# PEER block of a hybrid layer: 44 of the down tiles beside top-k, 12 between the gate products with low parts on VectorE, 8 behind them

## The chip, the cores and the metric

One core of one Trainium2 chip. The metric is device time in microseconds (us), the median over several executions; the kernel before takes 3331.22 us (three runs, 3329.69 to 3335.95).

## What is computed

The program is two layers on 512 tokens of width 1024 (a mixer with a PEER layer, then attention with a mixture of experts). The change is within the PEER layer. The part of the reference that matters:

```python
q = (xt @ w_query).reshape(t, PEER_HEADS, PEER_DKEY)            # 8 heads, 2 x 128
s1 = einsum("thd,hkd->thk", q1, sub_keys_1); s2 = ...           # 128 keys each
v1, i1 = top_k(s1, 16); v2, i2 = top_k(s2, 16)
top_s, pos = top_k(v1[..., :, None] + v2[..., None, :], 16)     # 16 of 256 pairs a head
gate = softmax(top_s)                                           # 128 (expert, gate) pairs a token
act = gelu(einsum("td,thkd->thk", x, w_down[expert])) * gate    # 16384 experts
y = einsum("thk,thkd->td", act, w_up[expert])
```

## The kernel before

For the first 128 tokens the 128 pairs of a token are gathered one by one. For the other 384 (TD) the layer is computed densely: the 16384 experts are 128 tiles of 128 experts, and each down tile is the product of a 128x1024 block of w_down with the tokens, followed by a gelu. Half of these tiles (STEPS = 64) are computed ahead, in otherwise different stages, and are written to the DRAM tensor `early`; the other half is computed in the experts stage itself, which reads one early tile and one block of gates at each of its 64 steps. Full precision comes from splitting each operand in a rounded high part (ScalarE) and a low part (the difference), so a down tile costs 24 matmuls: 8 blocks of the inner dimension times hi*hi, hi*lo, lo*hi (`part` or `product`).

*Score stage* (`stage_retrieve`, L1164). TensorE computes 68 tiles in the order of the list `order`: 16 query tiles ("q"), in four units of four, with 6 down tiles ("e") after each of the first three units and 34 after the last, SCORED = 52 in all. ScalarE evicts a tile (L1342 query, L1347 gelu), and splits the tile four further on (L1323); GpSimd makes the low parts (L1264); SP loads the next tile when a low part is done and saves groups of four tiles to `early`. VectorE meanwhile does the top-k of each unit (L1402 to L1467). It needs ScalarE for an Exp (L1363), which stands behind the eviction of the tiles in `exp_at` and waits for the centred scores (L1443); the sums (L1419) follow in the next unit. After the product of tile TILES - 4 TensorE transposes the picks for the next stage (L1316).

*Gates stage* (`stage_gate_matrix`, L1479). From the picks a matrix of gates, experts by tokens, is made for every token: VectorE writes two sets of 128x128 rows (L1517, one instruction for the four tokens of a group; L1520, three instructions; the fourth is made by ScalarE, L1575 distance and L1581 tent), TensorE multiplies them (L1544) into one of four banks of PSUM, ScalarE takes the bank to `out` (L1588). 16 groups make a batch (a 4 MB store by SP, L1645), and there are six batches with two buffers. Between the products 12 down tiles are computed, two in each batch: four of the tile's 24 matmuls (L1555) in each group but the first four; split (L1570) and gelu (L1566) on ScalarE, low part on GpSimd (L1530), the load at L1624, the save of the gelu's result at L1628. Four of the early tiles are loaded to `c.hid` at the start (L1632) for the first steps of the experts stage, with two blocks of w_up and of w_down.

*Experts stage* (`stage_peer_experts`, L1654). Its first matmul (L1749) waits for the split (L1792) and the low part (L1871) of its first tile.

A stage ends when SP has waited for all its transfers; the semaphores are then cleared behind a barrier of all engines (`Stage.__exit__`). An engine executes in the order of its program, and a wait holds all that is behind it. The semaphores of the change: `wd_h` counts splits, `wd_l` low parts, `h_done` finished tiles, `gelued` gelus, `taken` banks taken to `out`, `g_done` groups multiplied, `saved` and `stashed` finished stores.

## Time and profile before

| | |
|---|---|
| median of the runs | 3331.22 us |
| the profiled execution's own span | 3332.1 us |
| TensorE busy | 3127.5 us (94%) |
| VectorE busy | 2668.2 us (80%) |
| ScalarE busy | 1817.5 us (55%) |
| GpSimd busy | 834.3 us (25%) |
| score stage | about 554 to 876 us |
| gates stage | about 881 to 1054 us |
| experts stage | about 1055 to 1850 us |

In the profile PE is TensorE's matmuls, PEld its weight loads, DVE VectorE, ACT ScalarE, POOL GpSimd, SP the queue that issues most transfers; L1520 is line 1520 of the kernel. A name such as gates_hot is a tile of the program, `out<-in` names what an instruction writes and reads. Busy shares are means over stages with different bounds; a change in one stage is read from that stage.

### The profile page before, as it was taken

Reading aid. Unit: us, or ns where it says so; the run is one execution under the profiler, and the core shown is the slowest. Engines: PE = TensorE matmul, PEld = TensorE weight load, DVE = VectorE, ACT = ScalarE, POOL = GpSimd, SP = SyncE. Lnnn points to the kernel's source line nnn. Section 1 sums busy time; section 2 is a strip of 40 time slices with the busy share of each in tenths; the row PEclk is TensorE's granted clock in tenths of the full one; section 3 lists DMA queues with packets and bytes.
Section 4 is the critical chain, followed back from the end, with each engine's and each line's share of the span. In section 5 each row is a group of like instructions: output and inputs, shape, how many; then the busy total and the mean of one; then the engine's idle time right before and its main releaser. Section 6 shows DMA issues by size and latency. Waiting matters only on the chain. (4 is left out here: it accounts for less than half of the span.)

```text
span 3332.1 us, 47952 instructions
## 1 busy us (share of the span) xinstructions
PE 3127.5 (94%) x16376; PEld 2708.8 (81%) x16376; DVE 2668.2 (80%) x3821; ACT 1817.5 (55%) x2211; POOL 834.3 (25%) x516
## 2 busy tenths in 40 slices
PE   7999788999887999999999888799999999999998
PEld 7996677999887888888888766688888888888885
DVE  6895652995496887878888565899999999999997
ACT  4433442334585333333333344578877777877775
POOL 0000102445321444445545100211211211211212
PEclk9999888999998999999999889899999999999999
DMA  5231031335456998999998414699999999999996
GB/s 142 70 83 39 1 127 64 136 119 175 152 228 250 337 343 320 350 341 331 344 358 318 170 29 165 257 364 356 366 368 354 361 371 363 364 373 367 365 371 252
DMA packets 195750, 853.24 MB, mean 256 GB/s; under 512 B 21776, under 2 KB 104336, under 8 KB 151936
## 3 DMA queue, kind: packets, MB, share of 16 engines
q1 hardware_dynamic: 167712, 700.86, 57.4%
q0 software_dynamic: 27936, 151.02, 11.1%
q8 instruction: 64, 1.05, 0.1%
q14 instruction: 38, 0.31, 0.0%
HBM read 810.39 MB, written 59.24 MB: 261 GB/s over the span
## 5 line engine op out<-in xcount | busy, mean ns | idle before, releaser
L3207 DVE TENSOR_TENSOR moe_w_lo<-all_raw,moe_w_hi 128x2048 fp32r<-128x2048 f32 x298 | 676.2, 2287 | 50.6 <-ACT moe_w_hi L3133 48.2
L3133 ACT ACTIVATE moe_w_hi<-all_raw 128x2048 fp32r<-128x2048 f32 x298 | 569.3, 1916 | 80.0 <-PE moe_GU L3072 60.0
L3072 PE MATMUL moe_GU<-moe_w_hi,moe_x_lo 128*128 128x512 f32 x1056 | 412.3, 390 | 0.0
L3071 PE MATMUL moe_GU<-moe_w_lo,moe_x_hi 128*128 128x512 f32 x1056 | 412.2, 390 | 0.0
L3070 PE MATMUL moe_GU<-moe_w_hi,moe_x_hi 128*128 128x512 f32 x1056 | 411.7, 390 | 0.0
L1889 DVE SCALAR_TENSOR_TENSOR experts_pair<-experts_pair,all_x_first 128x1024 f32<-128x1024 f32 x128 | 156.4, 1222 | 142.6 <-DMA experts_pair<-in_peer_pairs,experts_slot 142.6
L1733 POOL DMA_INDIRECT experts_pair<-in_peer_pairs,experts_slot x128 | 222.4, 1738 | 114.7 <-POOL experts_slot L1730 110.0
L1264 POOL TENSOR_TENSOR score_w_lo<-all_hT,score_w_hi 128x1024 fp32r<-128x1024 f32 x67 | 165.2, 2467 | 303.7 <-DVE all_x_lo L1380 161.4
L1730 POOL COPY experts_slot<-all_pair_id 128x1 uint32 x128 | 152.8, 1194 | 334.1 <-DVE all_h L1901 304.4
L2976 POOL DMA_INDIRECT pair_rows<-all_mixT,all_slot x32 | 48.8, 1526 | 738.2 <-ACT all_mixT L3175 738.2
L3071 PEld LDWEIGHTS moe_GU<-moe_w_lo,moe_x_hi 128*128 128x128 f32 x1056 | 198.6, 188 | 42.1
L3072 PEld LDWEIGHTS moe_GU<-moe_w_hi,moe_x_lo 128*128 128x128 f32 x1056 | 198.6, 188 | 41.7
L3070 PEld LDWEIGHTS moe_GU<-moe_w_hi,moe_x_hi 128*128 128x128 f32 x1056 | 199.0, 188 | 40.6
L3207 DVE TENSOR_TENSOR moe_w_lo<-all_hT,moe_w_hi 128x2048 fp32r<-128x2048 f32 x98 | 222.5, 2284 | 0.1
L3080 PE MATMUL moe_Y<-moe_w_hi,moe_hid_hi 128*128 128x512 f32 x528 | 212.3, 402 | 0.8 <-DVE moe_hid_lo L3237 0.8
L3082 PE MATMUL moe_Y<-moe_w_hi,moe_hid_lo 128*128 128x512 f32 x528 | 206.2, 391 | 0.0
L3081 PE MATMUL moe_Y<-moe_w_lo,moe_hid_hi 128*128 128x512 f32 x528 | 205.8, 390 | 0.0
L3133 ACT ACTIVATE moe_w_hi<-all_hT 128x2048 fp32r<-128x2048 f32 x98 | 187.7, 1915 | 32.5 <-PE moe_GU L3072 18.7
L1749 PE MATMUL experts_H<-all_x_hi,experts_wd_hi 128*128 128x384 f32 x512 | 173.6, 339 | 20.0 <-DVE experts_wd_lo L1871 19.9
L1288 PE MATMUL score_H<-all_x_hi,score_w_hi 128*128 128x384 f32 (+1 forms) x544 | 190.3, 350 | 1.4 <-DVE all_x_lo L1380 1.4
L1290 PE MATMUL score_H<-all_x_hi,score_w_lo 128*128 128x384 f32 (+1 forms) x544 | 189.6, 349 | 0.0
L1289 PE MATMUL score_H<-all_x_lo,score_w_hi 128*128 128x384 f32 (+1 forms) x544 | 189.6, 349 | 0.0
(546 smaller groups left out, 8108.7 us busy)
## 6 DMA issues: line engine op xcount, KB each, us to landing
all_raw<-in_w_moe SPq DMA_DIRECT2D x149, 2048.0 KB, 9.8
all_hT<-in_w_moe SPq DMA_DIRECT2D x49, 2048.0 KB, 9.7
all_hT<-in_peer_wdT SPq DMA_DIRECT2D x128, 512.0 KB, 8.8
all_wu<-in_peer_pairs SPq DMA_DIRECT2D x64, 1024.0 KB, 10.5
peer_gates<-gates_out SPq DMA_DIRECT2D x6, 4096.0 KB, 11.6
experts_gt<-peer_gates SPq DMA_DIRECT2D x32, 768.0 KB, 9.7
all_hT<-in_w_in SPq DMA_DIRECT2D x40, 512.0 KB, 3.8
all_hid<-peer_early SPq DMA_DIRECT2D x60, 192.0 KB, 7.6
```

The lines of the kernel that those rows point to most:

```text
L1288: pe.matmul(out, left, c.x_hi[:, k, at:T], start=(k == 0), stop=False)
L1289: pe.matmul(out, left, c.x_lo[:, k, at:T], start=False, stop=False)
L1290: mm = pe.matmul(out, low, c.x_hi[:, k, at:T], start=False, stop=(k == KD - 1))
L1733: pool.indirect_dma_start(out=pair[:, v, :], out_offset=None, in_=a["peer_pairs"][:, :], in_offset=bass.IndirectOffsetOnAxis(ap=slot[:, n: ...
L3070: pe.matmul(out, x_hi[:, kx, :], hi[:, k, :], start=False, stop=False)
L3071: pe.matmul(out, x_hi[:, kx, :], lo[:, k, :], start=False, stop=False)
L3072: mm = pe.matmul(out, x_lo[:, kx, :], hi[:, k, :], start=False, stop=(kx == KD - 1))
L3080: pe.matmul(Y[:, b, :], hid_hi[:, h, :], hi[:, f, cols], start=(h == 0), stop=False)
L3081: pe.matmul(Y[:, b, :], hid_hi[:, h, :], lo[:, f, cols], start=False, stop=False)
L3082: mm = pe.matmul(Y[:, b, :], hid_lo[:, h, :], hi[:, f, cols], start=False, stop=(h == KD - 1))
L3133: act.activation(w_hi[p % RING][:], piece_of(r, p), ACT.Copy).then_inc(w_high, 1)
L3207: dve.tensor_tensor(w_lo[p % RING][:], piece_of(r, p), w_hi[p % RING][:].bitcast(F32), ALU.subtract).then_inc(w_low, 1)
```

## The change

SCORED falls from 52 to 44, so the score stage has 60 tiles, and the third and fourth Exp stand at tiles 39 and 47 in place of 43 and 56. The first four early tiles (DIRECT) are no longer computed there but last of all, in the gates stage, where their gelus write `c.hid` itself; the load of `c.hid` is gone.

In the gates stage 12 tiles are still computed between the group products (LOOPED), now six matmuls in each odd group and none in the even ones. Their low parts are made by VectorE, after the hot rows of groups 5 and 13 of each batch, but the very first, which stays on GpSimd. ScalarE's program is unrolled; a gelu and a split stand after take 0 and after take 8 of each batch. SP issues a load ahead of the saves of the batch before, and one behind them.

Behind the last group's products come 8 tiles more (TAIL), 24 matmuls each in one piece. Their raw weights are loaded during the last batch, six of them to the part of `out` that holds the last but one batch, once that is stored; four gelus go to what is left of it and are saved, four stay in `c.hid`. The store of the last batch is issued behind these loads and behind the saves of tiles 10 and 11.

```diff
-SCORED = 52
+SCORED = 44
+DIRECT = 4
-    exp_at = {18: 0, 29: 1, 43: 2, 56: 3}
+    exp_at = {18: 0, 29: 1, 39: 2, 47: 3}
-                    sp.dma_start(w[:, i % R, :], (wq_d if kind == "q" else wd_d)[n]).then_inc(w_in[i % R], 16)
+                    sp.dma_start(w[:, i % R, :], wq_d[n] if kind == "q" else wd_d[DIRECT + n]).then_inc(w_in[i % R], 16)
-                    sp.dma_start(c.early[g * G:(g + 1) * G].rearrange("j p t -> p j t"), stash[:, g % 2, :, :]).then_inc(stashed[g % 2], 16)
+                    sp.dma_start(c.early[DIRECT + g * G:DIRECT + (g + 1) * G].rearrange("j p t -> p j t"), stash[:, g % 2, :, :]).then_inc(stashed[g % 2], 16)
...
-    assert SCORED + 2 * BATCHES == STEPS and 2 * 3 * KD == 4 * (TB // U - R)
+    LOOPED, TAIL = 2 * BATCHES, 8
+    TILES = LOOPED + TAIL
+    FIRST = DIRECT + SCORED
+    KEPT = TILES - DIRECT
+    assert FIRST + LOOPED + TAIL - DIRECT == STEPS and 2 * 3 * KD == 6 * (TB // U) // 2 and BATCHES % 2 == 0
...
+        spare = out[:, 0, :, :].rearrange("p i t -> p (i t)")
+        queued = spare[:, 0:(TAIL - 2) * D].rearrange("p (j n) -> p j n", n=D)
+        kept = spare[:, (TAIL - 2) * D:(TAIL - 2) * D + DIRECT * TD].rearrange("p (j t) -> p j t", t=TD)
...
+        def tile(t):
+            return FIRST + t if t < KEPT else t - KEPT
+
+        def raw(t):
+            return wd[:, t % 2, :] if t < LOOPED + 2 else queued[:, t - LOOPED - 2, :]
+
+        def bent(t):
+            if t < LOOPED:
+                return stash[:, t % 2, :]
+            return kept[:, t - LOOPED, :] if t < KEPT else c.hid[:, t - KEPT, :]
...
-                with dve.Fori(0, TD // (R * U)) as it:
-                    for u in range(R):
-                        at = dve.snap(it * (R * U) + u * U)
-                        dve.wait_ge(g_done, it * R + (u + 1))
+                with dve.Fori(0, BATCHES) as b:
+                    for g in range(per * R):
+                        u = g % R
+                        at = dve.snap(b * TB + g * U)
+                        dve.wait_ge(g_done, b * (per * R) + (g + 1))
...
+                        if g == 5:
+                            dve.wait_ge(wd_h, b * 2 + 2)
+                            low(1, wd[:, 1, :])
+                        if g == 13:
+                            dve.wait_ge(wd_h, b * 2 + 3)
+                            low(0, wd[:, 0, :])
+                for t in range(LOOPED + 1, TILES):
+                    dve.wait_ge(wd_h, t + 1)
+                    low(t % 2, raw(t))
...
-                with pool.Fori(0, BATCHES) as b:
-                    for v in range(2):
-                        pool.wait_ge(wd_h, b * 2 + (v + 1))
-                        pool.wait_ge(gelued, b * 2 + (v + 1))
-                        pool.tensor_tensor(wd_lo[:, v, :], wd[:, v, :], wd_hi[:, v, :].bitcast(F32),
-                                           ALU.subtract).then_inc(wd_l, 1)
+                pool.wait_ge(wd_h, 1)
+                pool.tensor_tensor(wd_lo[:, 0, :], wd[:, 0, :], wd_hi[:, 0, :].bitcast(F32), ALU.subtract).then_inc(first_l, 1)
...
-                    for i in range(per):
-                        for u in range(R):
-                            n = b * (per * R) + (i * R + u)
...
-                            if i == 0:
-                                continue
-                            for q in range(4 * (R * (i - 1) + u), 4 * (R * (i - 1) + u) + 4):
-                                v, k, kind = q // (3 * KD), q // 3 % KD, q % 3
-                                if q % (3 * KD) == 0:
-                                    pe.wait_ge(wd_l, b * 2 + (v + 1))
-                                    pe.wait_ge(gelued, b * 2 + (v + 1))
...
-                                    mm.then_inc(h_done, 1)
+                    for g in range(per * R):
+                        u = g % R
+                        n = b * (per * R) + g
+                        pe.wait_ge(weighed, n + 1)
+                        pe.wait_ge(tented, n + 1)
+                        pe.wait_ge(taken, n + 1)
...
+                        mm.then_inc(g_done, 1)
+                        if g % 2 == 0:
+                            continue
+                        v = g // 8
+                        if g % 8 == 1:
+                            pe.wait_ge(first_l, 1)
+                            pe.wait_ge(wd_l, b * 2 + (v + 1))
+                            pe.wait_ge(gelued, b * 2 + (v + 1))
+                        for q in range(6 * (g % 8 // 2), 6 * (g % 8 // 2) + 6):
+                            mm = part(v, q)
+                        if g % 8 == 7:
+                            mm.then_inc(h_done, 1)
+                for t in range(LOOPED, TILES):
+                    pe.wait_ge(wd_l, t + 1)
+                    pe.wait_ge(gelued, t + 1)
+                    for q in range(3 * KD):
+                        mm = part(t % 2, q)
+                    mm.then_inc(h_done, 1)
...
                 def early(t):
                     act.wait_ge(h_done, t + 1)
-                    if t >= 2:
+                    if 2 <= t < LOOPED:
                         act.wait_ge(stashed[t % 2], 16 * (t // 2))
-                    act.activation(stash[:, t % 2, :], H[:, t % 2, 0:TD], ACT.Gelu).then_inc(gelued, 1)
+                    if t == LOOPED:
+                        act.wait_ge(saved[0], 16 * (BATCHES // 2))
+                    act.activation(bent(t), H[:, t % 2, 0:TD], ACT.Gelu).then_inc(gelued, 1)
...
+                    if t < LOOPED + 2:
+                        act.wait_ge(wd_in[t % 2], 16 * (t // 2 + 1))
+                    else:
+                        act.wait_ge(tail_in[t - LOOPED - 2], 16)
+                    act.activation(wd_hi[:, t % 2, :], raw(t), ACT.Copy).then_inc(wd_h, 1)
...
+                def take(b, g):
+                    n = R * per * b + g
+                    act.wait_ge(g_done, n + (R + 1))
+                    act.activation(out[:, b % 2, :, g * U:g * U + U],
+                                   ps[:, g % R, :, :].rearrange("p t i -> p i t"), ACT.Copy).then_inc(taken, 1)
+                    if n + R + 1 < ALL:
+                        distance(n + R + 1)
+                    if n + R < ALL:
+                        tent(n + R)
...
+                split(0)
                 for b in range(BATCHES):
-                    if b >= 1:
-                        early(2 * b - 2)
-                    split(2 * b)
                     if b >= 2:
                         act.wait_ge(saved[b % 2], 16 * (b // 2))
-                    take(b, 0)
-                    if b >= 1:
-                        early(2 * b - 1)
-                    split(2 * b + 1)
-                    if b < BATCHES - 1:
-                        with act.Fori(1, per) as q:
-                            take(b, q)
-                    else:
-                        for q in range(1, per):
-                            take(b, q, R * (per - q))
-                early(2 * BATCHES - 2)
-                early(2 * BATCHES - 1)
+                    for g in range(per * R):
+                        take(b, g)
+                        if g == 0:
+                            if b >= 1:
+                                early(2 * b - 1)
+                            split(2 * b + 1)
+                        if g == 8:
+                            early(2 * b)
+                            split(2 * b + 2)
+                early(LOOPED - 1)
+                split(LOOPED + 1)
+                for t in range(LOOPED, TILES):
+                    early(t)
+                    if t + 2 < TILES:
+                        split(t + 2)
...
                 def load(t):
-                    sp.dma_start(wd[:, t % 2, :], wd_d[SCORED + t]).then_inc(wd_in[t % 2], 16)
+                    if t == 2:
+                        sp.wait_ge(first_l, 1)
+                    elif t > 2:
+                        sp.wait_ge(wd_l, t - 1)
+                    sp.dma_start(raw(t), wd_d[tile(t)]).then_inc(wd_in[t % 2], 16)
...
                 def save(t):
                     sp.wait_ge(gelued, t + 3)
-                    sp.dma_start(c.early[SCORED + t], stash[:, t % 2, :]).then_inc(stashed[t % 2], 16)
+                    if t < LOOPED:
+                        sp.dma_start(c.early[tile(t)], bent(t)).then_inc(stashed[t % 2], 16)
+                    else:
+                        sp.dma_start(c.early[tile(t)], bent(t)).then_inc(tail_saved, 16)
...
-                sp.dma_start(c.hid[:], c.early[0:4].rearrange("j p t -> p j t")).then_inc(ahead, 16)
...
                 for b in range(BATCHES):
+                    load(2 * b + 2)
                     if b >= 1:
                         save(2 * b - 2)
                         save(2 * b - 1)
-                    if b + 1 < BATCHES:
-                        for v in range(2):
-                            sp.wait_ge(wd_l, 2 * b + v + 1)
-                            load(2 * b + v + 2)
+                    load(2 * b + 3)
+                    if b == BATCHES - 1:
+                        sp.wait_ge(saved[0], 16 * (BATCHES // 2))
+                        for t in range(LOOPED + 2, TILES):
+                            sp.dma_start(raw(t), wd_d[tile(t)]).then_inc(tail_in[t - LOOPED - 2], 16)
+                        save(LOOPED - 2)
+                        save(LOOPED - 1)
                     sp.wait_ge(taken, R * per * (b + 1) + R)
                     sp.dma_start(c.gates[b], out[:, b % 2, :, :].rearrange("p i t -> p (i t)")).then_inc(saved[b % 2], 16)
-                save(2 * BATCHES - 2)
-                save(2 * BATCHES - 1)
+                for t in range(LOOPED, KEPT):
+                    save(t)
                 for b in range(2):
                     sp.wait_ge(saved[b], 16 * (BATCHES // 2))
                     sp.wait_ge(stashed[b], 16 * BATCHES)
-                sp.wait_ge(ahead, 16 * 5)
+                sp.wait_ge(tail_saved, 16 * DIRECT)
+                sp.wait_ge(ahead, 16 * 4)
```

## Rows read from the trace of the kernel before

**Rows 1.** The head of the profile's page.

```profile
span 3332.1 us, 47952 instructions
```

**Rows 2.** Windows: us, then busy of PE, PEld, DVE, ACT, POOL, clock, DMA share, GB/s.

```profile
800.00:850.00 50.00, 50.00 (x290) 50.00 (x289) 12.60 (x14) 20.24 (x28) 29.97 (x13) 1.00 0.50 173
...
937.37:963.45 26.08, 23.18 (x179) 22.67 (x178) 26.08 (x65) 22.16 (x53) 5.35 (x2) 1.00 0.55 216
...
1075.00:1843.00 768.00, 764.65 (x3697) 673.05 (x3697) 620.01 (x859) 276.69 (x432) 364.08 (x244) 1.00 0.92 339
```

**Rows 3.** Timeline, ScalarE, end of score: start, us, instruction, idle before it.

```profile
871.69 0.49 ACT L1347 ACTIVATE score_stash<-score_H 128x384 f32<-128x384 f32 x1 [3.67 <-PE score_H L1290]
...
875.85 0.49 ACT L1347 ACTIVATE score_stash<-score_H 128x384 f32<-128x384 f32 x1 [2.52 <-PE score_H L1290]
```

**Rows 4.** Waits in the gates stage: waited for in all, times, longest.

```profile
PE gates_ps L1544 <- DVE gates_hot L1520: 24.3, 14, 7.0
```

**Rows 5.** Timeline from the last group of gates to the experts stage.

```profile
1037.03 0.85 DVE L1520 TENSOR_SCALAR gates_hot<-all_count,all_idxT 128x128 f32<-128x128 f32 x3
...
1039.78 1.05 PE L1544 MATMUL gates_ps<-gates_hot 128*128 128x128 f32 x8
...
1041.19 0.34 PE L1555 MATMUL gates_H<-all_x_hi,gates_wd_lo 128*128 128x384 f32 x1
...
1055.03 1.06 ACT L1792 ACTIVATE experts_wd_hi<-all_hT 128x1024 fp32r<-128x1024 f32 x1 [12.80 <-SPq L1706]
...
1057.40 0.69 PE L1749 MATMUL experts_H<-all_x_hi,experts_wd_hi 128*128 128x384 f32 x1 [15.87 <-DVE experts_wd_lo L1871]
```

**Rows 6.** Timeline of the top-k's last unit, with the evictions of tiles 43 and 56.

```profile
758.43 1.06 DVE L1435 TENSOR_TENSOR score_cand<-score_v 128x384 f32<-128x384 f32 x2
...
775.02 0.49 ACT L1347 ACTIVATE score_stash<-score_H 128x384 f32<-128x384 f32 x1 [2.72 <-PE score_H L1290]
...
777.24 0.29 DVE L1419 TENSOR_REDUCE score_total<-score_gate 128x8 f32<-128x128 f32 x1 [17.75 <-ACT score_gate L1363]
...
786.85 0.55 DVE L1443 TENSOR_TENSOR score_gate<-score_best 128x128 f32<-128x128 f32 x1
...
809.18 0.29 DVE L1467 TENSOR_TENSOR score_pick<-score_eq 128x128 f32<-128x128 bf16 x1
...
829.10 0.49 ACT L1347 ACTIVATE score_stash<-score_H 128x384 f32<-128x384 f32 x1 [2.72 <-PE score_H L1290]
```

**Rows 7.** Timeline of VectorE in the third batch, and GpSimd's low part beside it.

```profile
943.87 0.68 DVE L1517 TENSOR_TENSOR gates_hot<-all_count,all_idxT 128x512 f32<-128x512 f32 x1
...
945.24 0.68 DVE L1517 TENSOR_TENSOR gates_hot<-all_count,all_idxT 128x512 f32<-128x512 f32 x1
...
945.37 2.79 POOL L1530 TENSOR_TENSOR gates_wd_lo<-all_hT,gates_wd_hi 128x1024 fp32r<-128x1024 f32 x1 [3.39 <-ACT gates_wd_hi L1570]
...
948.67 0.68 DVE L1517 TENSOR_TENSOR gates_hot<-all_count,all_idxT 128x512 f32<-128x512 f32 x1
```

**Rows 8.** Timeline of VectorE in the experts stage: low parts of this size.

```profile
1062.86 1.23 DVE L1871 TENSOR_TENSOR experts_wd_lo<-all_hT,experts_wd_hi 128x1024 fp32r<-128x1024 f32 x1
...
1064.00 1.22 DVE L1875 TENSOR_TENSOR experts_wu_lo<-all_wu,experts_wu_hi 128x1024 fp32r<-128x1024 f32 x1
```

**Rows 9.** Timeline of TensorE in the third batch: one group and its parts.

```profile
950.52 1.05 PE L1544 MATMUL gates_ps<-gates_hot 128*128 128x128 f32 x8
...
951.33 0.42 PE L1555 MATMUL gates_H<-all_x_lo,gates_wd_hi 128*128 128x384 f32 x1
...
952.11 1.05 PE L1544 MATMUL gates_ps<-gates_hot 128*128 128x128 f32 x8
```

**Rows 10.** DMA issues of the gates stage: count, KB each, median us to landing.

```profile
peer_gates<-gates_out SPq DMA_DIRECT2D x6, 4096.0 KB, 11.6
...
peer_early<-gates_stash SPq DMA_DIRECT2D x12, 192.0 KB, 11.0
```

**Rows 11.** Timeline, ScalarE, first instruction of the score stage.

```profile
542.70 1.06 ACT L1323 ACTIVATE score_w_hi<-all_hT 128x1024 fp32r<-128x1024 f32 x1 [1.19 <-PEq L66]
```

More of the change, by code:

```diff
@@ L1533, in _, with part @@
             @block.tensor
             def _(pe):
+                def part(v, q):
+                    k, kind = q // 3, q % 3
+                    left = (wd_lo if kind == 2 else wd_hi)[:, v, k * P:k * P + P]
+                    right = (c.x_lo if kind == 1 else c.x_hi)[:, k, P:T]
+                    return pe.matmul(H[:, v, 0:TD], left, right, start=(q == 0), stop=(q == 3 * KD - 1))
                 pe.sem_inc(g_done, R)
                 with pe.Fori(0, BATCHES) as b:
[L1537 to L1558 removed]
@@ new lines, in _ @@
+                    for g in range(per * R):
[4 more added lines that the diff above has]
+                        pe.wait_ge(taken, n + 1)
+                        for j in range(U):
+                            mm = pe.matmul(ps[:, u, j, :], hot[:, u, 1, j, :], hot[:, u, 0, j, :], start=True, stop=True)
+                        mm.then_inc(g_done, 1)
[10 more added lines that the diff above has]
+                            mm.then_inc(h_done, 1)
@@ L1570, in split, with distance @@
[L1570 to L1573 removed]
+                    if t < LOOPED + 2:
[3 more added lines that the diff above has]
+                    act.activation(wd_hi[:, t % 2, :], raw(t), ACT.Copy).then_inc(wd_h, 1)
+                def distance(n):
+                    if n >= 2:
@@ L1580, in tent @@
                     act.wait_ge(spread, n + 1)
-                    act.activation(hot[:, u % R, 0, U - 1, :], far[:, u % 2, :], ACT.Relu, scale=minus[:, ds(at, 1)],
-                                   bias=c.idxT[:, 2, ds(at, 1)]).then_inc(tented, 1)
-                def take(b, q, left=None):
-                    for u in range(R):
-                        n = q * R + (R * per * b + u)
-                        act.wait_ge(g_done, n + (R + 1))
-                        act.activation(out[:, b % 2, :, ds(q * (R * U) + u * U, U)],
-                                       ps[:, u, :, :].rearrange("p t i -> p i t"), ACT.Copy).then_inc(taken, 1)
-                        if left is None or u + R + 1 < left:
-                            distance(n + (R + 1), u + 1)
-                        if left is None or u + R < left:
-                            tent(n + R, u)
+                    act.activation(hot[:, n % R, 0, U - 1, :], far[:, n % 2, :], ACT.Relu, scale=minus[:, at:at + 1],
+                                   bias=c.idxT[:, 2, at:at + 1]).then_inc(tented, 1)
```

35 lines of the change are left out of this document (13 added, 22 removed).

## Prediction

> **What bounds the kernel now.** I read the page's head first, then a table of windows over the stages that the change touches, then the timeline at each seam of those stages. [rows 1] gives the profiled execution's span, 3332.1 us; the median of the runs is 3331.22 us, so the two differ by 0.03% and a difference taken from the span may be applied to the median as it stands.
>
> The change touches three stages. In the score stage TensorE is the bound: it is busy 50.00 of 50 us in 800 to 850, at full clock, while VectorE has all but done its work (12.60 us) [rows 2]. One down tile there costs the distance between two evictions, 875.85 - 871.69 = 4.16 us, which is 24 matmuls at 0.173 us [rows 3]. In the gates stage VectorE is the bound: in the batch from 937.37 to 963.45 it is busy 26.08 of 26.08 us, TensorE 23.18, ScalarE 22.16 [rows 2], and what TensorE waits for is the hot rows of VectorE (24.3 us in 14 waits, 7.0 of them the stage's start) [rows 4]. Batches repeat every 26.0 to 26.1 us. In the experts stage TensorE is again the bound: 764.65 of 768 us busy, clock 1.00 [rows 2]. Between gates and experts TensorE stands still: its last matmul begins at 1041.19 and the first of the next stage at 1057.40, 16.21 us later [rows 5]. So a tile moved out of one PE-bound stretch is worth 4.16 us, and pays 4.16 us where it lands, unless it lands on idle time.
>
> **Part 1: 8 tiles fewer in the score stage.** TILES falls from 68 to 60: 8 x 4.16 = 33.3 us less, if the top-k on VectorE doesn't become late. It has to deliver before the transposes after tile 56 (turn_at); both orders are equal up to tile 59, and tile 56 is evicted at 829.10 [rows 6]. Before, VectorE was idle from 758.43 + 1.06 to 777.24, because the third Exp stood at tile 43 (775.02) [rows 6]. It now stands at tile 39, four tiles earlier, 775.02 - 16.6 = 758.4: VectorE goes on some 2 us after that eviction, as it did before (775.02 to 777.24), about 17 us earlier. Its last selection (809.18) ends near 792.6, and the centred scores that the fourth Exp waits for (786.85) are there at about 770. That Exp now stands at tile 47, 829.10 - 9 x 4.16 = 791.7. ScalarE therefore waits at neither, and the picks are ready some 30 us ahead of need. If ScalarE did have to wait there, the evictions and splits queued behind it would stop TensorE; the margin is 21 us for the one and, for the other, the value it waits for precedes the row at 758.43 on its engine. Cost 0. The end of the stage (last save, barrier) is of the same form. Part 1: -33.3.
>
> **Part 2: the loop over gate products.** VectorE's pace is 1.37 us a group (943.87 to 945.24); the group after that takes 948.67 - 945.24 = 3.43 us while GpSimd's low part (2.79 us from 945.37) runs, a stall of 2.06 us [rows 7]. This pattern stands 12 times, and 16 x 1.37 + 2 x 2.06 = 26.0 is the batch, so nothing else holds it. The change takes 11 of 12 low parts from GpSimd (the first stays) and gives VectorE 12 of its own (tiles 1 to 12, two in each batch, after groups 5 and 13). The same instruction on VectorE in the experts stage takes 1.14 us from start to next start (1062.86 to 1064.00) [rows 8]. So -11 x 2.06 + 12 x 1.14 = -22.7 + 13.7 = -9.0. Bounds for one such low part in this stage: 1.14 (that row) and 2.06 (no better than the stall it replaces: then the part is worth +2.1 in sum). I take 1.14 since it is the same operation, size and types.
>
> The trace shows VectorE starting an instruction 0.08 us before the one ahead has ended (1062.86 + 1.23 = 1064.09) [rows 8]. The Trainium skill, VectorE: DVE Perf Modes, section "The DRAIN you can't avoid", says that the next op doesn't start until the pipe is empty. By that the low parts would cost their full 1.23 and the sum would be 1 us smaller; this row speaks for the overlap.
>
> Is VectorE then still the bound? TensorE spends 0.81 us on a group's products (950.52 to 951.33) and 0.78 on four parts, the first 0.26 and then 0.173 each [rows 9]. Now even groups have no part (0.9 us, an estimate: eight at the same pace to the next start), odd groups six: 0.81 + 0.26 + 5 x 0.173 = 1.94. A pair is 2.84, a batch 22.7 us. VectorE: 16 x 1.37 + 2 x 1.14 = 24.2. ScalarE: its 22.16 us a batch of now [rows 2] stay, as the same takes, distances, tents, two splits and two gelus. VectorE stays the bound, by 1.5 us.
> New waits: VectorE waits at its low parts for the split of that tile; behind the wait stand the next groups' hot rows, for which TensorE waits. ScalarE splits after take 0 and take 8, some 3 us before VectorE comes by after groups 5 and 13; nothing waits. In the first batch TensorE waits for the one GpSimd low part, as VectorE leads by up to four groups this falls into its slack. ScalarE's part is unrolled instead of looped: cost 0, the last batch was unrolled before, and its evictions still kept up with TensorE.
> End of the loop: TensorE lagged VectorE: the last hot rows end at 1037.03 + 0.85 = 1037.88, the last group starts at 1039.78 and the last part at 1041.19, 3.31 after [rows 5]. Now TensorE catches up in the pause that VectorE's low part after group 13 makes, so the last part starts 0.81 + 0.26 + 4 x 0.173 = 1.77 after: -1.5 (bounds 0 and -1.9). Part 2: -10.5.
>
> **SP's queue in the loop.** The load of tile 2b+2 is now issued right behind the 4 MB store of gates, with two saves after it. A save issued 1 us behind that store lands in 11.0 us (the store takes 11.6) [rows 10], so transfers on this queue land in order: load at about 11.6 + 1.5 = 13.1 us after the store's issue (512 KB at the store's 353 KB/us), save near 13.6. The store is issued after take 15 and ScalarE wants both after take 8, nine takes later: 9 x 1.37 + 1.14 for the low part between = 13.5, up to 14.2 us with an odd group's lag. The margin is half a us; past it ScalarE has some 3 us (of the group 8 to group 13 distance on VectorE, 5 x 1.37, less take, gelu and split) before VectorE's wait after group 13 stalls. Cost 0; bounds 0 and 5 batches x 1 us, were it to hit the engines at once. In the last batch six loads (3 MB, 9 us) and the wait for the fifth store stand ahead of saves 10, 11 and the last store; save 11 waits for the last looped gelu, so the store goes out some 1 to 2 us later than the takes would allow. That is hidden by part 3.
>
> **Part 3: 8 tiles at the end.** 8 x 4.16 = +33.3 on TensorE, [rows 3]. Beside it: each tile's split and low part (1.06 + 1.14) behind the gelu (0.49) of the tile two before is 2.8 us with the hand-overs, against 4.16 of the product that covers it: hidden with 1.3 us to spare. The last store (12 us) and the save of the last written tile, issued 16 us before the end, lie under these 33 us. The four tiles kept on chip save one 768 KB load at the stage's start, which nothing waited for: 0.
>
> **Part 4: the seam.** Before, 16.21 us from last part to first matmul. Now: matmul 0.34, gelu 0.49 [rows 3], clearing and barrier, split 1.06 + 0.03, low part 1.23 + 0.04. The barrier: at the seam ahead of the score stage ScalarE sat idle 1.19 us for it [rows 11]; here a store issued right behind the last part (1041.19 + 0.34) and landing 11.6 later leaves 1.9 us until ScalarE starts at 1055.03 [rows 5, 10]. I take 1.4, nearer to the row that shows the seam alone. Sum 0.34 + 0.49 + 1.4 + 1.09 + 1.27 = 4.6: -11.6 (bounds -11.8 and -11.1). What is late next is the same split and low part.
>
> **Sum.** -33.3 - 10.5 + 33.3 - 11.6 = -22.1 us, on the span 3310.0, on the median 3309.1.
>
> **Rivals.**
> (a) The loop keeps its time: a low part on VectorE costs as much as the stall, or TensorE and VectorE hand over worse in pairs of 0.9 and 1.94 us. For it: only 1.5 us between the two engines. Against: four groups of buffers, and the pause falls on the leading engine. Then only the seam counts, with the end of the loop: 3331.2 - 11.6 - 1.5 = 3318. Chance 0.15.
> (b) The tail is bound by its chain. If split and low part of a tile didn't overlap with the product before it, 7 x 2.8 = 20 us come back: 3329. Against: two buffers of each kind, and ScalarE and VectorE idle there otherwise. Chance 0.06.
> (c) The change doesn't hide the last store: something at the stage's end still waits for it or for a save. The order on SP puts store and saves 16 us or more before the end; if it failed the seam's 11.6 would be lost: 3321. Chance 0.03.
> (d) Slower: ScalarE waits at take 8 for the load behind the store. It costs nothing up to about 17 us after the store's issue; from there each us costs one in each of 5 batches. To lose the 22 gained and 6.7 more it must land 23 us after the issue, where the rows give 13.6. Price at 24 us: 5 x 7 = 35, so 3344. Chance 0.03.
> (e) Forecast: 3309.1, own range 3304 to 3314 (low part 1.14 to 1.5, barrier 1.2 to 1.9, ScalarE 0 to 1 us a batch). Chance 0.73.
>
> **How the numbers follow.** Range 3304 to 3318, which takes in (a); outside lie (b), (c), (d) and a little of (e). What a measurement can tell from no change is 0.2%, 6.7 us. Faster: (e), (a) and (c), 0.91. Same: (b), 0.06. Slower: (d), 0.03.
>
> **What would show it.** After: gates batches of 24.2 to 24.5 us with VectorE busy throughout and no stalled hot row but one; last score eviction near 842.6; a tail with gelus every 4.16 us; 4 to 5 us from its last matmul to the first of experts; experts of the same length. Wrong would be: batches at 26, a ScalarE wait for wd or stash, TensorE waits in the tail, or an experts stage that is longer by what was gained.

## The result, and the profile after

The changed kernel takes 3308.31 us (median of four runs, 3299.80 to 3317.34) where the kernel before takes 3333.59 us (four runs, 3329.69 to 3336.48): a ratio of 0.9929, 95% interval 0.9909 to 0.995. (The ratios given here and below are estimates from the runs of both kernels; they differ by up to 0.0006 from the quotient of the two medians, which is 0.9924 here.) The forecast was 3309.1 of 3331.22, a ratio of 0.9934. That the median hits it within 1 us is luck: the four runs lie 17.5 us apart. The profiled execution is the slowest of the four, with a span of 3315.6 us; where its extra length lies stands below.

Head of the profile of after; what answers to it is [rows 1]:

```profile
span 3315.6 us, 47588 instructions
...
PE 3132.8 (94%) x16376; PEld 2712.2 (82%) x16376; DVE 2670.2 (81%) x3840; ACT 1818.4 (55%) x2211; POOL 780.3 (24%) x497
```

TensorE has nearly the same work as before (3132.8 us busy, before 3127.5) in a shorter span; GpSimd has 54 us less. A whole execution can't show where 22 us went, since executions of one kernel differ by nearly as much. So I cut the trace at events that both kernels have: first and last gelu of the score stage, first and last hot row of VectorE, last down part (the third matmul of a part), first matmul of experts, last matmul of experts. All columns are differences of such starts, in us:

| | score gelus | to hot rows | hot rows | to last part | seam | **stretch** | experts |
|---|---|---|---|---|---|---|---|
| before | 292.9 | 5.5 | 156.2 | 3.6 | 16.2 | **474.5** | 800.7 |
| after | 259.6 | 5.6 | 147.2 | 35.6 | 4.4 | **452.4** | 802.3 |
| after, again | 259.7 | 5.5 | 147.1 | 35.8 | 4.4 | **452.5** | 795.1 |
| after, third | 259.6 | 5.6 | 147.1 | 35.6 | 4.4 | **452.3** | 798.7 |

The "stretch", from the first gelu of score to the first matmul of experts, holds the whole change. It is 22.1 us shorter (474.47 to 452.36), as forecast, and repeats within 0.2 us; the experts stage behind it, which the change doesn't touch, varies by 7 us between executions of one kernel. Each part: score -33.3 (forecast -33.3), hot rows -9.0 (-9.0), from the last hot row to the last part +31.9 (+33.3 - 1.5), seam -11.8 (-11.6), and +0.1 at the stage's start.

Windows of after (us, busy of PE, PEld, DVE, ACT, POOL, clock, DMA share, GB/s), which answer to [rows 2]: two stretches of the loop and the tail:

```profile
881.00:905.00 24.00, 24.00 (x189) 23.81 (x188) 24.00 (x67) 22.15 (x54) 0.00 (x0) 1.00 0.61 235
...
928.00:952.00 24.00, 23.53 (x176) 22.51 (x176) 24.00 (x67) 22.09 (x54) 0.00 (x0) 1.00 0.61 235
1001.00:1034.00 33.00, 32.77 (x190) 32.45 (x188) 8.58 (x7) 10.29 (x16) 0.00 (x0) 1.00 0.38 157
```

VectorE is still the bound of the loop (24.00 of 24.00 us busy in both), TensorE close behind, GpSimd at nothing; in the tail TensorE is the bound. From VectorE's first hot row of a batch to that of the next it is 26.50 us for the first batch and then 24.19 to 24.20; before it was 26.21 and then 26.05 to 26.08.

Timeline of VectorE and GpSimd in after, which answers to [rows 7, 8]: the one low part that stayed on GpSimd, and one of the twelve on VectorE:

```profile
854.77 0.68 DVE L1549 TENSOR_TENSOR gates_hot<-all_count,all_idxT 128x512 f32<-128x512 f32 x1
855.28 2.38 POOL L1568 TENSOR_TENSOR gates_wd_lo<-all_hT,gates_wd_hi 128x1024 fp32r<-128x1024 f32 x1 [23.89 <-ACT gates_wd_hi L1622]
855.38 2.88 DVE L1552 TENSOR_SCALAR gates_hot<-all_count,all_idxT 128x128 f32<-128x128 f32 x3
...
858.18 0.67 DVE L1549 TENSOR_TENSOR gates_hot<-all_count,all_idxT 128x512 f32<-128x512 f32 x1
...
921.67 1.21 DVE L1540 TENSOR_TENSOR gates_wd_lo<-all_hT,gates_wd_hi 128x1024 fp32r<-128x1024 f32 x1
922.80 0.67 DVE L1549 TENSOR_TENSOR gates_hot<-all_count,all_idxT 128x512 f32<-128x512 f32 x1
```

The group beside GpSimd takes 858.18 - 854.77 = 3.41 us instead of 1.37, as every such group did before; the low part on VectorE takes 922.80 - 921.67 = 1.13. The first batch holds both kinds, 2.04 + 2 x 1.13 = 4.3 us beside its hot rows, and so gains nothing: 26.5 against 26.21.

Timeline of the tail and the seam in after (start, us, instruction, idle before it), which answers to [rows 5]:

```profile
1025.48 0.49 ACT L1615 ACTIVATE all_hid<-gates_H 128x384 f32<-128x384 f32 x1 [2.72 <-PE gates_H L1576]
1025.87 1.05 ACT L1622 ACTIVATE gates_wd_hi<-gates_out 128x1024 fp32r<-128x1024 f32 x1
1029.64 0.49 ACT L1615 ACTIVATE all_hid<-gates_H 128x384 f32<-128x384 f32 x1 [2.72 <-PE gates_H L1576]
...
1033.43 0.34 PE L1576 MATMUL gates_H<-all_x_hi,gates_wd_lo 128*128 128x384 f32 x1
1033.81 0.49 ACT L1615 ACTIVATE all_hid<-gates_H 128x384 f32<-128x384 f32 x1 [3.67 <-PE gates_H L1576]
1035.45 1.06 ACT L1855 ACTIVATE experts_wd_hi<-all_hT 128x1024 fp32r<-128x1024 f32 x1 [1.15 <-SPq L1769]
...
1036.54 1.22 DVE L1934 TENSOR_TENSOR experts_wd_lo<-all_hT,experts_wd_hi 128x1024 fp32r<-128x1024 f32 x1 [8.36 <-ACT experts_wd_hi L1855]
...
1037.82 0.69 PE L1812 MATMUL experts_H<-all_x_hi,experts_wd_hi 128*128 128x384 f32 x1 [4.05 <-DVE experts_wd_lo L1934]
```

The nine gelus from 1000.52 to 1033.81 stand 4.16 us apart, and the splits of the tail each follow right behind one. The last store was issued at 1001.42, more than 30 us before the stage's last gelu, so ScalarE's 12.80 us of idle time in [rows 5] has become 1.15. What is left of the seam is what the forecast named: barrier, split, low part.

Windows in the experts stage, the same stretch of two executions, after and after again:

```profile
1100.00:1400.00 300.00, 297.40 (x1438) 261.50 (x1437) 240.78 (x334) 107.91 (x168) 139.31 (x96) 1.00 0.91 334
```

```profile
1100.00:1400.00 300.00, 300.00 (x1454) 264.85 (x1453) 242.22 (x334) 107.00 (x168) 145.59 (x96) 1.00 0.92 341
```

Same code, same clock, but TensorE pauses for 2.6 us in the one and never in the other. (Before: 297.84 busy in this stretch.) Over the whole experts stage it waited eight times in the one, 5.2 us in all, each time for a low part of VectorE (L1934), never in the other, and four times, 2.3 us in all, in the third. The spans of the first two differ by 8.5 us and their experts stages by 7.2, so most of the profiled execution's extra length lies there. Why VectorE was late in some executions only, no run shows.

### The profile page after: what moved, and what is told of

Its sections match the earlier page's. It is cut to its first block and busy times, and to the rows that moved or that the text cites. A ratio compares the mean times of both kernels' runs of the same rounds, so it can differ in the third digit from the quotient of the medians.

```text
span 3315.6 us, 47588 instructions
## 1 busy us (share of the span) xinstructions
PE 3132.8 (94%) x16376; PEld 2712.2 (82%) x16376; DVE 2670.2 (81%) x3840; ACT 1818.4 (55%) x2211; POOL 780.3 (24%) x497
## 3 DMA queue, kind: packets, MB, share of 16 engines
q0 software_dynamic: 27936, 151.02, 11.2%
## 5 line engine op out<-in xcount | busy, mean ns | idle before, releaser
L1265 POOL TENSOR_TENSOR score_w_lo<-all_hT,score_w_hi 128x1024 fp32r<-128x1024 f32 x59 | 146.0, 2476 | 292.1 <-DVE all_x_lo L1381 163.9
L1814 PE MATMUL experts_H<-all_x_hi,experts_wd_lo 128*128 128x384 f32 x512 | 172.7, 337 | 0.0
L1813 PE MATMUL experts_H<-all_x_lo,experts_wd_hi 128*128 128x384 f32 x512 | 172.4, 337 | 0.0
L1289 PE MATMUL score_H<-all_x_hi,score_w_hi 128*128 128x384 f32 (+1 forms) x480 | 168.8, 352 | 1.4 <-DVE all_x_lo L1381 1.4
## 6 DMA issues: line engine op xcount, KB each, us to landing
peer_gates<-gates_out SPq DMA_DIRECT2D x6, 4096.0 KB, 12.1
```

Of the source, the lines that this page charges most:

```text
L1813: pe.matmul(out, hi, c.x_lo[:, k, P:T], start=False, stop=False)
L1814: mm = pe.matmul(out, lo, c.x_hi[:, k, P:T], start=False, stop=(k == KD - 1))
```

## The experiments

The experiments take the rivals (a) to (d) of the prediction in turn. All kernels compute the whole result; diffs are against after, shortened where "..." stands. The first four kernels ran beside the kernel before, which took 3328.83 us there (19 runs). Where one run is all there is, the whole time can't settle differences of some us, and the reading rests on the stretch in its trace.

**The same kernel once more.**

> The changed kernel once more, as the measure for the variants beside it. The stretch from the score stage's first gelu to the first matmul of the experts stage took 474.5 us in the profile before and 452.3 after (1057.4 - 582.9, 1037.8 - 585.5). If the -22.2 us belong to the change and what differs before and behind it (2.6 + 3.1 us) is the executions' own spread, the stretch is 452 us again within 0.5, and the span differs by some us from the 3315.6 of the first profile. Rival: the extra 5.7 us outside the stretch are caused by the change (longer loops, other addresses); then they stand there again.

Measured: 3308.44 us, ratio 0.9945 (0.9928 to 0.9962); stretch 452.5. It shows the noise, above.

**Low parts of the loop back on GpSimd, all else as in after.**

```diff
+                with pool.Fori(0, BATCHES) as b:
+                    for v in (1, 0):
+                        pool.wait_ge(wd_h, b * 2 + (3 - v))
+                        pool.tensor_tensor(wd_lo[:, v, :], wd[:, v, :], wd_hi[:, v, :].bitcast(F32),
+                                           ALU.subtract).then_inc(wd_l, 1)
...
-                        if g == 5:
-                            dve.wait_ge(wd_h, b * 2 + 2)
-                            low(1, wd[:, 1, :])
-                        if g == 13:
-                            dve.wait_ge(wd_h, b * 2 + 3)
-                            low(0, wd[:, 0, :])
...
```

> The 12 low parts of the loop back on GpSimd, everything else as changed. Theory (VectorE is the loop's bound, and a GpSimd low part stalls it for 2.06 us where its own costs 1.14): 12 x (2.06 - 1.14) = 11 us more in the loop, less nothing else: the stretch from the first gelu to the experts' first matmul 463 us, batches of 26.0. Rival (the loop is bound by the hand-over between TensorE and VectorE and the gain came from the other distribution of the 24 matmuls): stretch 452 to 455, batches of 23.5 to 24.2 as now.

Measured: 3317.63 us, 0.9969 (0.996 to 0.9979). Hot rows 158.4 against after's 147.2, the columns around them as in after within 0.1 us: stretch 463.6. From the second on, batches are back at 26.08 to 26.14 us; the first, with three low parts on GpSimd, took 28.12. Timeline of VectorE and GpSimd:

```profile
949.37 0.70 DVE L1548 TENSOR_TENSOR gates_hot<-all_count,all_idxT 128x512 f32<-128x512 f32 x1
949.93 2.38 POOL L1567 TENSOR_TENSOR gates_wd_lo<-all_hT,gates_wd_hi 128x1024 fp32r<-128x1024 f32 x1 [10.66 <-ACT gates_wd_hi L1622]
949.97 2.43 DVE L1551 TENSOR_SCALAR gates_hot<-all_count,all_idxT 128x128 f32<-128x128 f32 x1
```

One tensor_scalar that takes 0.33 us elsewhere takes 2.43 and ends within 0.1 us of GpSimd's instruction (952.40 and 952.31): a stall of 2.10 us, against 1.13 for doing the work itself. So rival (a) falls, and the loop's gain is the stall's, not the new order of the parts. The Trainium skill, SBUF — State Buffer, "SBUF: two separate sides", says that the port pair which GpSimd shares with some of VectorE's instructions is an exclusive lock held for a whole instruction; this row agrees.

**No tail: 52 tiles in score, none behind the loop, the last store at the end.**

```diff
-SCORED = 44
-DIRECT = 4
+SCORED = 52
+DIRECT = 0
-    LOOPED, TAIL = 2 * BATCHES, 8
+    LOOPED, TAIL = 2 * BATCHES, 0
...
```

With them go what hangs on them: the Exps stand at tiles 43 and 56 and `c.hid` is loaded at the start, as before the change.

> The loop part alone: 52 tiles beside top-k as before, no tiles behind the last group, four early tiles loaded as before, low parts on VectorE. Theory: the loop's gain of 9.0 + 1.5 stays and the seam stands at 16.2 us again: stretch 474.5 - 10.5 = 464 us, less or more 1 (one superfluous split and low part in the last batch costs 1.1), VectorE from first to last hot row 147.6. Rival (the tail is what gains and the loop would pay as much without it): 470 or more.

Measured: 3318.4 us, 0.9971 (0.9961 to 0.9981). Score 292.9, hot rows 147.0, to last part 2.5, seam 15.9, stretch 463.8: the loop's part alone, 10.7 us. The kernel with its low parts on GpSimd keeps the other half, 474.5 - 463.6 = 10.9 us. The two halves add up to 21.6 of after's 22.1, so they hardly interact.

**Four tiles in the tail.**

```diff
-SCORED = 44
+SCORED = 48
-    LOOPED, TAIL = 2 * BATCHES, 8
+    LOOPED, TAIL = 2 * BATCHES, 4
...
-                sp.wait_ge(tail_saved, 16 * DIRECT)
```

All four tiles of the tail stay in `c.hid`, so it has no saves.

> Four tiles at the end instead of eight, 48 beside top-k. Theory: a tile is worth 4.16 us wherever TensorE is the bound, and four (16.6 us) still cover the last store (some 12 us) that is issued 1.5 us after the last part: stretch 452.3, seam 4.2 us, no difference. Rival (the store together with the queue behind it needs more cover than 16.6 us): the seam grows, to 8 us or more.

Measured: 3307.84 us, 0.9943 (0.9925 to 0.996). Score 276.3, to last part 19.1, seam 4.4, stretch 452.3, the same as with eight. Moving a tile costs 4.16 us where it lands and saves 4.16 us where it left; only the cover of the store counts, and four tiles (16.6 us) are enough here: the last store was issued at 1017.76 and landed 11.3 us later, 4.0 us before the last part. That speaks against rival (c) too: the seam is 15.9 without cover and 4.4 with either.

**The tail in series: each split only after the gelu of the tile before it.**

```diff
                 for t in range(LOOPED, TILES):
                     early(t)
-                    if t + 2 < TILES:
-                        split(t + 2)
+                    if LOOPED < t and t + 1 < TILES:
+                        split(t + 1)
```

> In the tail ScalarE splits a tile only behind the gelu of the tile just ahead of it, so split and low part no longer lie under a product. It prices the rival in which the chain binds the tail. Forecast: 6 tiles (14 to 19) each wait for gelu 0.49 + split 1.05 + low part 1.23 and the hand-overs, 2.8 us: gelus 7.0 us apart instead of 4.16, tail 17 us longer, stretch 469. If the tail had slack of another kind (the raw tiles' loads late, SP's queue), it would grow by less than 17.

Measured: 3340.52 us in one run; to last part 64.0, stretch 480.7, so 28.4 us more than after where 17 were expected. Timeline of one tile, then the window:

```profile
1015.59 0.49 ACT L1615 ACTIVATE gates_out<-gates_H 128x384 f32<-128x384 f32 x1 [7.35 <-PE gates_H L1576]
1015.98 1.05 ACT L1622 ACTIVATE gates_wd_hi<-gates_out 128x1024 fp32r<-128x1024 f32 x1
...
1017.06 1.22 DVE L1540 TENSOR_TENSOR gates_wd_lo<-gates_out,gates_wd_hi 128x1024 fp32r<-128x1024 f32 x1 [7.56 <-ACT gates_wd_hi L1622]
1018.34 0.44 PE L1576 MATMUL gates_H<-all_x_hi,gates_wd_hi 128*128 128x384 f32 x1 [2.78 <-DVE gates_wd_lo L1540]
...
1020.20 0.52 PE L1576 MATMUL gates_H<-all_x_hi,gates_wd_hi 128*128 128x384 f32 x1
1020.52 0.52 PE L1576 MATMUL gates_H<-all_x_lo,gates_wd_hi 128*128 128x384 f32 x1
```

```profile
1004.00:1060.00 56.00, 39.29 (x160) 37.29 (x159) 7.35 (x6) 8.61 (x12) 0.00 (x0) 0.79 0.15 61
```

The idle time per tile is as forecast, 2.78 us. What was not: the granted clock, 1.00 in after's tail, is 0.79 here, and part of each tile's matmuls stand 0.32 us apart, the pace at 1.2 GHz, instead of 0.173 at 2.4. The trace adds up: six idle times of 2.78 us make 16.7; from first to last matmul the six tiles take 5.66, 5.69, 5.44, 5.70, 6.83 and 5.40 us instead of 3.99 each, 10.8 us more; and the last matmul ahead of each idle time now runs to its end with none behind it, some 0.17 us six times. Together these are the 28.4, within 0.2. The chain is as I described it, and after doesn't run into it (TensorE has no wait in its tail). But the price of rival (b), 20 us for seven tiles, was too low: at 28.4 for six, seven would cost some 33 (an estimate).

**The transfers behind the store, made late.** Three kernels put an extra store of 1, 2 or 4 MB to scratch space behind the store of each of the first five batches. This tests the claim of half a us of margin and 3 us of slack on SP's queue. The diff is that of 2 MB; with 1 MB it is half of x_hi, with 4 MB a second store, of x_lo, follows.

```diff
                     sp.dma_start(c.gates[b], out[:, b % 2, :, :].rearrange("p i t -> p (i t)")).then_inc(saved[b % 2], 16)
+                    if b < BATCHES - 1:
+                        sp.dma_start(more[b, 0, :, 0:KD, :], c.x_hi[:].bitcast(F32)).then_inc(extra, 16)
```

> A further store of 1 MB (the high parts of x to a scratch tensor) right behind each of the first five stores of gates, ahead of the load and the saves. Rule of the forecast: load and save behind the store land at 13.6 + 2.9 = 16.5 us after the store's issue, ScalarE wants them after some 13.5 to 14.2 and has 3 us more before VectorE or TensorE feel it: stretch unchanged, 452 to 453, ScalarE waits for stash some 2 to 3 us in each batch. Rival (ScalarE's wait is passed on at once): 5 x 2.9 = 14 us more.

> The same with 2 MB: landing at 13.6 + 5.8 = 19.4 us. By the rule of the forecast (free up to 17) 5 x 2.4 = 12 us more, stretch 464. Rival (passed on at once): 5 x 5.3 = 27 more. Rival (no loss, the slack is the whole batch): 452.

> The same with 4 MB: landing at 25.2 us. By the rule 5 x 8.2 = 41 us more, stretch 493. The step from the 2 MB kernel to this one should be 5 x 5.8 = 29 us if the batch is then bound by the landing.

Measured in one run each: 3317.49, 3331.0 and 3354.97 us (before 3324.68 there); stretches 462.9, 477.0 and 503.0, which is 10.6, 24.7 and 50.6 us above after where 0, 12 and 41 were expected. The step from 2 to 4 MB, 26 us in five batches, is near the 29 expected; the point from which it costs is what I had wrong. Waits of the gates stage with 1 MB (waited for in all, times, longest):

```profile
DVE gates_wd_lo L1542 <- ACT gates_wd_hi L1624: 31.4, 12, 5.4
...
ACT gates_stash L1617 <- DMA peer_early<-gates_stash: 17.8, 5, 4.2
...
PE gates_ps L1589 <- ACT gates_hot L1635: 9.5, 5, 2.5
```

The path is the one I named: ScalarE's gelu after take 8 waits for the save, and VectorE for the split behind it. (Of VectorE's twelve waits seven stand in the tail, where after has them too; the five in the loop add up to 8.4 us.) TensorE also waits, for the tents of ScalarE, which I hadn't named. How much slack there is can be read in after itself, ScalarE, VectorE and SP's queue in the third batch:

```profile
904.22 0.33 SPq L1707 DMA_DIRECT2D peer_gates<-gates_out  x1
...
918.82 0.49 ACT L1615 ACTIVATE gates_stash<-gates_H 128x384 f32<-128x384 f32 x1 [0.85 <-DMA peer_early<-gates_stash]
919.21 1.05 ACT L1622 ACTIVATE gates_wd_hi<-all_hT 128x1024 fp32r<-128x1024 f32 x1
...
920.90 0.84 DVE L1552 TENSOR_SCALAR gates_hot<-all_count,all_idxT 128x128 f32<-128x128 f32 x3
```

ScalarE starts as the save lands, 918.82 - 904.22 = 14.6 us after the store's issue, where 13.6 were forecast, and has by then waited 0.85 us. Its split ends at 920.26, and VectorE comes by at 921.67: 1.4 us of slack are left, not some 3. The batches differ: ScalarE waits 0.99, 0.85, 0.10, 0.00 and 0.21 us for the save in the second to the sixth, and 0.73, 1.41, 2.13, 2.37 and 2.03 us are left behind its split.

With 1 MB more the gelu starts 16.7 to 17.3 us after the store's issue, 2.1 to 2.7 us later than in after, and VectorE now waits for the split in each of the five batches, 1.30, 1.86, 2.07, 1.63 and 1.56 us. In the third batch:

```profile
923.41 1.23 DVE L1542 TENSOR_TENSOR gates_wd_lo<-all_hT,gates_wd_hi 128x1024 fp32r<-128x1024 f32 x1 [1.86 <-ACT gates_wd_hi L1624]
```

In the second batch the cost is what after's slack leaves, 16.74 - 14.61 - 0.73 = 1.40 us. In the later ones it is more than that: the larger slack which after has there isn't found once a batch has been late. The gelu's start less VectorE's wait says where the cost begins, 15.1 to 15.4 us after the store's issue in all five batches. The batches grow by 9.0 us in sum, and 1.6 more stand behind VectorE's last hot row; TensorE had waited 2.2 us for a tent shortly before it. The granted clock in stretches of this loop fell too, to 0.93 in 905 to 929 us, where after has 1.00; what that costs here was not separated.

**The queue turned round.** If order on the queue is the cause, then a save and a load issued ahead of the store remove it, whatever the store's size.

```diff
+                load(2)
                 for b in range(BATCHES):
-                    load(2 * b + 2)
                     if b >= 1:
-                        save(2 * b - 2)
                         save(2 * b - 1)
                     ...
+                    if b < BATCHES - 1:
+                        save(2 * b)
+                        load(2 * b + 4)
                     sp.wait_ge(taken, R * per * (b + 1) + R)
                     sp.dma_start(c.gates[b], ...)
```

> SP's queue turned: the save of tile 2b-2 and the load of tile 2b+2 are issued ahead of the store of batch b-1 instead of behind it. In the changed kernel ScalarE waits 0.9 to 1.0 us after take 8 for the save (14.6 us after the store's issue), and this is swallowed. Theory: that wait goes, and nothing else: stretch 452.3 (within 0.5), the ScalarE waits for stash gone, since 1.4 us of slack took them. Rival (the waits cost something in each batch): stretch 448 to 450.

> The turned queue with the 2 MB store behind each of the first five stores, which cost 24.7 us in the kernel as changed (stretch 477.0). Theory (those 24.7 us are the save and the load that land behind the stores, through ScalarE's wait after take 8 and VectorE's after group 13): with both ahead of the stores the cost goes, stretch 452 to 454. Rival (it is the transfers' own load on memory or on the engines' reads): 470 to 477.

Measured: order alone 3307.95 us (ratio 0.9939, 0.9919 to 0.9958), stretch 452.5, nothing gained. ScalarE's waits for the save are gone, as expected, and they had cost nothing. Order with the 2 MB: 3305.55 us in one run where the 2 MB alone took 3331.0; the stretch is 452.5 again instead of 477.0. Issues of the gates stage (count, KB each, median us to landing), first of the kernel with 2 MB, then with the queue turned:

```profile
peer_more<-all_x_hi SPq DMA_DIRECT2D x5, 2048.0 KB, 16.7
...
peer_early<-gates_stash SPq DMA_DIRECT2D x12, 192.0 KB, 16.6
```

```profile
peer_early<-gates_stash SPq DMA_DIRECT2D x12, 192.0 KB, 8.0
```

The medians mix the two saves of a batch. With the queue turned the one that ScalarE waited for is issued ahead of the store and lands 1.9 to 5.4 us later, long before it is wanted; the other, behind the stores, takes 14.4 to 14.8 us, and ScalarE is never held by it. And ScalarE's gelu of the third batch, with 2 MB and then with 2 MB and the queue turned:

```profile
926.94 0.49 ACT L1617 ACTIVATE gates_stash<-gates_H 128x384 f32<-128x384 f32 x1 [5.73 <-DMA peer_early<-gates_stash]
```

```profile
917.44 0.47 ACT L1617 ACTIVATE gates_stash<-gates_H 128x384 f32<-128x384 f32 x1
```

The wait of 5.73 us is gone with the same bytes moved, so what cost was the place in the queue and not the traffic.

**A version with what is left.** It has the queue turned, the first low part on VectorE too (after group 3), and the first split and low part of the experts stage made in the tail, into buffers that both stages share.

```diff
-        wd_hi, wd_lo = (s.sb(f"wd_{n}", [P, 2, D], F32R) for n in ("hi", "lo"))
+        wd_hi, wd_lo = c.wd_hi, c.wd_lo
...
+                    if g == 3:
+                        dve.wait_ge(wd_h, 1)
+                        low(0, wd[:, 0, :])
...
+                dve.wait_ge(wd_h, TILES + 1)
+                low(TILES % 2, late[:, 0, :])
...
+                    if t == TILES - 2:
+                        act.wait_ge(ahead, 16 * 4)
+                        act.activation(wd_hi[:, 0, :], late[:, 0, :], ACT.Copy).then_inc(wd_h, 1)
...
```

> The changed kernel with three things more: the queue turned as in the run before; the first low part on VectorE instead of GpSimd (after group 3; 2.04 - 1.14 = 0.9 us less); the split and low part of the experts stage's first tile made in the tail, under the last product, in buffers that both stages share, and that of its second tile ahead of the wait for gates (the seam 4.4 - 2.3 = 2.1 us, and 1 us less wait before the second tile). Forecast: stretch 452.3 - 0.9 - 2.3 = 449.1; the experts stage 1 us shorter from its first matmul. In all -4 us or 0.12% against the changed kernel: the trace can show it, the times hardly. Rival (the seam's floor is the barrier and another wait comes last there): stretch 451 or more.

> The changed kernel beside the one before this, on the same chip: stretch 452.3 to 452.5 for the third time; time 20 to 25 us under that of the kernel before.

Measured side by side: 3302.26 us (0.9916, 0.99 to 0.9932) against 3309.38 for after (0.9934, 0.9916 to 0.9953) and 3329.38 for before. In the traces the stretch is 449.2 against 452.3, as forecast: hot rows 146.5 (147.1), seam 2.1 (4.4). The timeline of the seam:

```profile
1032.17 0.49 ACT L1635 ACTIVATE all_hid<-gates_H 128x384 f32<-128x384 f32 x1 [2.73 <-PE gates_H L1596]
1033.88 0.44 PE L1837 MATMUL experts_H<-all_x_hi,all_wd_hi 128*128 128x384 f32 x1 [1.74 <-DVEq L2017]
```

Only the last gelu and the barrier stand between the stages now. The 3.1 us are shown by the traces; the two intervals overlap, so the medians alone don't separate the kernels. The 1 us that the experts stage was to gain can't be told: it took 794.1 us, where three executions of after spread over 7.

## Why the prediction was right, and where it wasn't

- What bounds each stage: right. TensorE in the score stage and the tail, VectorE in the loop.
- Part 1: right, -33.3 for -33.3. ScalarE doesn't wait for the top-k: in after's score stage it waits for TensorE and for one load only.
- Part 2, the loop: right, -9.0 for -9.0. The pace of VectorE in [rows 7], the stall as a difference of two starts, and the low part's 1.14 us from another stage [rows 8] carried it to a tenth. The end of the loop moved by -1.4 for -1.5: the last looped part starts 1.9 us after the end of the last hot rows, not 1.77. Undoing the twelve low parts gave 11.2 us back, 12 x (2.06 - 1.13). Of the signs that would have shown it wrong one did appear, a ScalarE wait for stash; it reached no other engine. A low part takes 1.13 us from start to start at a duration of 1.21. The Trainium skill, VectorE: DVE Perf Modes, "The DRAIN you can't avoid", has the next op wait until the pipe is empty, and goes on that a next op which is not held starts earlier. The prediction left that out: its row [rows 8] and this one, 0.08 us earlier than the end, fit the exception and don't speak against the section.
- SP's queue: the cost of 0 was right, but the step behind it was mis-sized and the verdict had less room than it says. The save landed 14.5 us after the store's issue, not 13.6: the store took 12.1 us in after instead of 11.6, and the load behind it landed 1.9 us after the store (at 14.0, not 13.1) instead of 1.5. The "half a us of margin" was none: ScalarE waited in four of five batches, up to 1.0 us. And the slack behind its wait, 3 us in the forecast, was 0.7 to 2.4 us, 2.35 at most with the queue turned, where ScalarE waits for nothing. I had counted only take, gelu and split between group 8 and group 13; ScalarE is busy 22.1 of 24 us, which leaves it little time to catch up. Rival (d)'s "up to about 17 us" was some 15 once a batch had been late, and its price of 35 us at 24 stands against 50.6 measured with the gelu at 24.1 to 24.3. Each us past that point does cost about one in each of five batches, as said: 26 us between 2 and 4 MB for some 5 us later. That all of this lay hidden in the changed kernel was in part luck: in its second batch 0.7 us were left.
- Part 3: right. The chain of a tile of 2.8 us lies beside 4.16 us of products, and the isolated chain measured 2.78. Its price if it had not been hidden was wrong: rival (b) takes 2.8 us a tile, and 4.7 were measured, because the clock falls too. I priced idle time and left out that matmuls after it may run slower.
- Part 4: right, -11.8 for -11.6. The barrier took 1.15 us and not the 1.4 I chose; [rows 11], the other end of that bound, had 1.19.
- "Experts of the same length" can't be confirmed to better than the spread: 795.1 to 802.3 in three executions of after, 800.7 in one of before.

## What to carry to other kernels

When two engines share work, compare the helper's real price, read as the distance between two starts on the engine that it disturbs, with doing the work on that engine: 2.04 to 2.10 us against 1.13 here. A store at the end of a stage is covered by any independent work as long as itself (here 16.6 us of it did for a store of 11 to 12 us what 33.3 do), and moving more of it is neutral. On a transfer queue issue the small things that are wanted soon ahead of the large store, even where it brings nothing yet: it took away a cost of 24.5 us that one more store of 2 MB behind each of five batches had made.

## What the runs showed of the hardware that I had not expected

Idle gaps of 2.8 us before each tile of 24 matmuls brought TensorE's granted clock from 1.00 to 0.79, with matmuls 0.32 us apart instead of 0.173 in part of every tile, so that 17 us of idle time cost 28. The slow matmuls did not always begin right behind the gap: in two of the six tiles five to seven matmuls first stood 0.17 to 0.20 us apart. After the seam the clock falls as well, but for one short stretch: 0.60 in the first 6.2 us of experts in after, 0.72 in the version with a seam of 2.1 us, and 1.00 behind it in both, as far as 1100 us. ScalarE, idle 2 us of 24, passed on 1.3 to 2.1 us of a delay of 2.1 to 2.7 us to VectorE.
